# First two feed-forward layers: eight of 22 gate/up pairs as 2x2 blocks in seven products

## The reference

```
def swiglu(x, wi, wo):
    gate, up = jnp.split(x @ wi, 2, axis=-1)
    return (jax.nn.silu(gate) * up) @ wo
...
h = h + 0.5 * swiglu(rms_norm(h, ffn1_norm[li]), ffn1_wi[li], ffn1_wo[li])
```

## Time and profile before

| | us |
|---|---|
| median of 3 runs | 2762.38 (2761.88 to 2763.02) |
| the profiled execution | 2763.58, its span 2761.8 |
| PE busy | 2717.8 (98%), 14176 matmuls |
| PEld busy | 2210.9 (80%) |
| DVE busy | 1572.0 (57%) |
| ACT busy | 1205.9 (44%) |
| POOL busy | 622.4 (23%) |
| all loads | 255 MB, 92 GB/s over the span |

### The profile page before, as it was taken

The page is one execution under the profiler, slowest core; times in us unless marked ns, Lnnn a source line. Parts: engine busy times, 40 slices in busy tenths (PEclk is TensorE's granted clock), DMA queues, the critical chain, the costliest instruction groups (busy, mean ns, idle before and its releaser), DMA issues.

```text
span 2761.8 us, 39016 instructions
## 1 busy us (share of the span) xinstructions
PE 2717.8 (98%) x14176; PEld 2210.9 (80%) x14176; DVE 1572.0 (57%) x2421; ACT 1205.9 (44%) x1814; POOL 622.4 (23%) x607
## 2 busy tenths in 40 slices
PE   8999999999999999999999999999999999899998
PEld 6888888788888888887778888877888888777777
DVE  5444336544443575435965764348777777676664
ACT  4333232543322333223553333246655555457775
POOL 3000013100001351002733520013322222123232
PEclk9999999999999999999999999999999999999999
DMA  5333332233333464333204653322222222122222
GB/s 151 92 99 93 99 83 77 80 96 92 98 98 93 143 189 133 93 99 90 77 26 120 188 154 95 97 70 76 70 70 70 70 71 67 43 77 62 68 61 69
DMA packets 484827, 255.24 MB, mean 92 GB/s; under 512 B 17843, under 2 KB 478422, under 8 KB 484710
## 3 DMA queue, kind: packets, MB, share of 16 engines
q1 hardware_dynamic: 484534, 253.40, 32.0%
q10 hardware_dynamic: 176, 0.27, 0.0%
HBM read 251.51 MB, written 2.13 MB: 92 GB/s over the span
## 4 chain that ended last, share of the span: by engine, by line
PE 91%; DVE 6%; ACT 1%; POOL 1%; issue 1%; DMA 0%; DVEq 0%; SPq 0%; ACTq 0%; POOLq 0%
PE bank L259 73%; PE bank L1906 2%; PE bank L1937 1%; PE bank L1939 1%; PE bank L1938 1%; DVE w_lo L245 1%; DVE dsa_work L1603 1%; PE bank L2013 1%; PE bank L2821 1%; DVE small L1597 1%; PE bank L2813 1%; PE bank L2050 1%; PE bank L2846 1%; DVE gdn_blocks L2410 1%; PE bank L981 1%
## 5 line engine op out<-in xcount | busy, mean ns | idle before, releaser
L259 PE MATMUL bank<-x_hi,w_hi 128*128 128x512 f32 x2320 | 936.6, 404 | 8.5 <-DVE w_lo L245 4.8
L259 PE MATMUL bank<-x_hi,w_lo 128*128 128x512 f32 x2320 | 907.7, 391 | 0.0
L259 PE MATMUL bank<-x_lo,w_hi 128*128 128x512 f32 x2320 | 906.7, 391 | 0.6 <-DVE x_lo L586 0.6
L245 DVE TENSOR_TENSOR w_lo<-w_raw,w_hi 128x1024 fp32r<-128x1024 f32 x429 | 529.9, 1237 | 551.4 <-ACT w_hi L239 550.8
L239 ACT ACTIVATE w_hi<-w_raw 128x1024 fp32r<-128x1024 f32 x429 | 450.6, 1055 | 615.9 <-PE bank L259 567.1
L259 PEld LDWEIGHTS bank<-x_hi,w_hi 128*128 128x128 f32 x2320 | 437.1, 188 | 106.4 <-issue 15.3
L259 PEld LDWEIGHTS bank<-x_hi,w_lo 128*128 128x128 f32 x2320 | 436.2, 188 | 93.2
L259 PEld LDWEIGHTS bank<-x_lo,w_hi 128*128 128x128 f32 x2320 | 437.6, 189 | 87.5 <-issue 3.6
L435 POOL TENSOR_TENSOR sumsq<-sumsq,sq 128x512 f32<-128x512 f32 x56 | 91.7, 1638 | 1290.6 <-ACT sq L421 1290.0
L259 PE MATMUL bank<-h_hi,w_hi 128*128 128x512 f32 x768 | 298.9, 389 | 0.0
L259 PE MATMUL bank<-h_hi,w_lo 128*128 128x512 f32 x768 | 298.8, 389 | 0.0
(11 more groups left out here) (485 smaller groups left out, 3471.8 us busy)
## 6 DMA issues: line engine op xcount, KB each, us to landing
w_raw<-in_ffn_wi_dram SPq DMA_DIRECT2D x176, 512.0 KB, 3.8
w_raw<-in_ffn_wo_dram SPq DMA_DIRECT2D x64, 512.0 KB, 3.7
w_raw<-in_ada_w_dram SPq DMA_DIRECT2D x48, 512.0 KB, 4.9
w_raw<-in_a_w_in_dram SPq DMA_DIRECT2D x48, 512.0 KB, 4.0
w_raw<-in_b_w_in_dram SPq DMA_DIRECT2D x32, 512.0 KB, 4.1
w_raw<-in_ffn_wo_dram SPq DMA_DIRECT2D x32, 384.0 KB, 3.2
w_raw<-in_even_w_in_dram SPq DMA_DIRECT2D x16, 512.0 KB, 4.0
w_raw<-in_a_w_out_dram SPq DMA_DIRECT2D x16, 512.0 KB, 3.5
```

Of the source, the lines that this page charges most:

```text
L245: dve.tensor_tensor(w_lo[s][:], w_raw[raw_of(b) % RAW][:], w_hi[s][:].bitcast(F32), ALU.subtract).then_inc(w_lo_done, 1)
L259: mm = pe.matmul(out, lhs[:, w], rhs(kt), start=first and kk == 0 and m == 0, stop=last and kk == len(kts) - 1 and m == 2)
```

## The change

In ffn0 and ffn1, pairs 6 to 13 of 22 (SEVEN_AT = 6, SEVEN_N = 8) are computed as a product of 2x2 blocks. The weight side is split into gate/up by lower/upper four k-tiles, the token side into lower/upper four k-tiles by the first and last 256 tokens (T1, T2). Instead of eight block products seven are run, each of 4 k-tiles x 3 matmuls of 128x128 by 256 tokens (`seven_group`), on sums and differences of blocks. PE's order in a steady turn n is: products 5 and 2 of pair n, product 3 of pair n-1 (`last_pe`), products 1 and 7 of pair n+1 (`first_pe`, `seventh_pe`), and products 4 and 6 of pair n.

The work round it: DVE makes x_part = hres x gain x rstd in eight operations in the first turn of the loop (`parts_dve`); POOL makes four sums of its quarters, ACT and DVE split them into t_hi and t_lo. x_hi and x_lo are themselves rewritten with the parts of x_part in four steps (`own_act`, `own_dve`), the first one from the middle of the last dense block on; rstd then becomes 1. For each pair POOL makes four sums of weight halves, 128x512 each: both, three (in place), low (in place), all. ACT and DVE split left, both and all (512 columns) and row and low (1024 columns). ACT copies products 1 and 7 out of the bank (256 columns each) and applies Silu in two halves; DVE joins partial sums in banks and in prod. The raw loads of pair n+2 wait for these (`seven_sp`). Six dense pairs stand in front and eight behind, the first of these split round the last product 3. In the seven stretch the loops are written out. Two pairs move in the order of h tiles (`seven_col`), which the down product reads by the same map. The core of the diff:

```diff
+SEVEN = (0, 1)
+SEVEN_AT, SEVEN_N = 6, 8
+HT = T // 2
...
+        x_part, x_sum = tile("x_part", 4, KT), tile("x_sum", FT + 4, KT)
+        t_hi = [tile(f"t_hi{c}", FT + 14 + 2 * c, 2, F32R) for c in range(4)]
+        t_lo = [tile(f"t_lo{c}", 14 + 2 * c, 2, F32R) for c in range(4)]
+        w_both, w_all = tile("w_both", 13), tile("w_all", FT + 13)
+        p7_copy = [sumsq[:, 0:HT], sumsq[:, HT:T]]
...
         def ffn_pe(pe, f, run, r, begun=0):
             b0, t0 = BASE[f"ffn{f}"]
-            if not ada_of(f):
+            if f in SEVEN:
...
+                project_pe(pe, run, b0, t0, 4, r, begun)
+                for u in range(4, 2 * SEVEN_AT - 1):
+                    one(u)
+                one(2 * SEVEN_AT - 1, part=0, half=upper_read)
+                one(2 * SEVEN_AT - 1, part=1)
+                seven_pe(pe, f, one)
+                o = 2 * (SEVEN_AT + SEVEN_N)
+                for u in range(1, 4):
+                    one(o + u)
+                with pe.Fori(1, (2 * FT - o) // 4) as i:
+                    for u in range(4):
+                        one(o + u, i, 4)
+            elif not ada_of(f):
...
                     dve.tensor_tensor(prod[s][:], prod[s][:], gate_s[s][:], ALU.mult).then_inc(prod_done, 1)
+                    if f in SEVEN and turn0 == 0:
+                        parts_dve(dve, f, gain, range(4 * s, 4 * s + 4))
...
+        def seven_sp(sp, f, n, src):
...
+                if n >= 2:
+                    if m == 0:
+                        sp.wait_ge(all_added, c + 1)
+                        sp.wait_ge(row_lo, c + 1)
+                    else:
+                        sp.wait_ge(low_lo, c + 1)
...
+        def parts_dve(dve, f, gain, ks):
+            for k in ks:
+                x = slice(k * T, k * T + T)
+                dve.scalar_tensor_tensor(x_part[:, x], hres[:, x], gain[:, k:k + 1], rstd[:], ALU.mult, ALU.mult).then_inc(part_made, 1)
...
+        def parts_pool(pool, f):
...
+            pool.tensor_tensor(s22, b22, b12, ALU.subtract).then_inc(part_added, 1)
+            pool.tensor_tensor(s12, b11, b12, ALU.subtract).then_inc(part_added, 1)
+            pool.wait_ge(part_added, c + 1)
+            pool.tensor_tensor(s11, s22, b11, ALU.add).then_inc(part_added, 1)
+            pool.wait_ge(part_added, c + 3)
+            pool.tensor_tensor(s21, s11, b21, ALU.subtract).then_inc(part_added, 1)
...
+        OWN = ((0, T1), (1, T1), (1, T2), (0, T2))
+        def own_act(act, f, m):
...
+            act.activation(quarter(x_hi, k, t), quarter(x_part, k, t), ACT.Copy).then_inc(own_hi, 1)
...
+        def seven_group(pe, slot, h, x, out, first=False):
+            hi, lo = w_hi[slot], w_lo[slot]
+            x_h, x_l = x
+            for k in range(4):
+                w = slice(h * T + k * P, h * T + k * P + P)
+                for m, (lhs, rhs) in enumerate(((hi, x_h), (hi, x_l), (lo, x_h))):
+                    mm = pe.matmul(out, lhs[:, w], rhs[:, k, :], start=first and k == 0 and m == 0, stop=k == 3 and m == 2, skip_group_check=True)
+            return mm
...
+        def seven_pe(pe, f, one):
+            seventh_pe(pe, f, 0)
+            first_pe(pe, f, 0)
+            seventh_pe(pe, f, 1)
+            for n in range(SEVEN_N):
...
+                seven_group(pe, slot_of(f, 0), 0, part_pair(2), B[:, T1])
...
+                seven_group(pe, slot_of(f, 0), 1, own_pair(1, T1), A[:, T1]).then_inc(p2_done, 1)
+                if n:
+                    last_pe(pe, f, n - 1)
+                if n + 1 < SEVEN_N:
+                    first_pe(pe, f, n + 1)
+                    if n:
+                        seventh_pe(pe, f, n + 1)
+                pe.wait_ge(low_lo, c + 1)
+                pe.wait_ge(p7_joined, c + 1)
...
+                seven_group(pe, slot_of(f, 3), 0, part_pair(1), B[:, T1])
+                seven_group(pe, slot_of(f, 3), 1, part_pair(3), B[:, T2]).then_inc(p4_done, 1)
...
+            own_pe(pe, f, 3)
+            one(o, part=0)
+            last_pe(pe, f, SEVEN_N - 1)
+            one(o, part=1)
...
+        def seven_act(act, f):
...
+            own_act(act, f, 0)
+            own_act(act, f, 1)
+            both_act(act, f, 1)
+            copy_act(act, f, 0)
+            left_act(act, f, 1)
+            low_act(act, f, 0)
+            own_act(act, f, 2)
+            for n in range(SEVEN_N):
+                if n + 1 < SEVEN_N:
+                    row_act(act, f, n + 1)
...
+                first_silu(act, f, n)
+                all_act(act, f, n)
+                if n == 0:
+                    own_act(act, f, 3)
+                if n:
+                    last_silu(act, f, n - 1)
+                if n + 2 < SEVEN_N:
+                    left_act(act, f, n + 2)
+                if n + 1 < SEVEN_N:
+                    copy_act(act, f, n + 1)
+                if n:
+                    seven_h_hi(act, f, n - 1)
+                if n + 1 < SEVEN_N:
+                    low_act(act, f, n + 1)
+                if n + 2 < SEVEN_N:
+                    both_act(act, f, n + 2)
+                if n == 0:
+                    high(1)
+            next_hi(act, f, 1)
+            last_silu(act, f, SEVEN_N - 1)
...
+        def last_dve(dve, f, n):
...
+            dve.wait_ge(p4_done, seven(f) + n + 1)
+            dve.tensor_tensor(prod[s][:, T2], B[:, T1], p7_copy[n % 2], ALU.add).then_inc(last_joined, 1)
...
+        def join_dve(dve, f, n):
...
+            dve.tensor_tensor(B[:, T2], B[:, T1], p7_copy[n % 2], ALU.add).then_inc(p7_joined, 1)
...
+        def seven_dve(dve, f):
...
+            both_dve(dve, f, 0)
+            own_dve(dve, f, 0)
+            up(1)
+            product(1)
+            both_dve(dve, f, 1)
+            own_dve(dve, f, 1)
+            left_dve(dve, f, 1)
+            for n in range(SEVEN_N):
+                if n:
+                    last_dve(dve, f, n - 1)
+                low_dve(dve, f, n)
+                if n and n + 1 < SEVEN_N:
+                    both_dve(dve, f, n + 1)
+                join_dve(dve, f, n)
+                if n + 1 < SEVEN_N:
+                    row_dve(dve, f, n + 1)
...
+                if n == 0:
+                    own_dve(dve, f, 2)
+                all_dve(dve, f, n)
+                if n:
+                    up_dve(dve, f, n - 1)
+                if n == 0:
+                    own_dve(dve, f, 3)
+                if n + 2 < SEVEN_N:
+                    left_dve(dve, f, n + 2)
+                if n == 0:
+                    low(1)
+                else:
+                    h_lo_dve(dve, f, n - 1)
...
+        def seven_pool(pool, f):
+            parts_pool(pool, f)
+            for n in range(2):
+                both_pool(pool, f, n)
+                three_pool(pool, f, n)
+                low_pool(pool, f, n)
+                if n == 0:
+                    all_pool(pool, f, 0)
+            for n in range(SEVEN_N - 1):
+                all_pool(pool, f, n + 1)
+                if n + 2 < SEVEN_N:
+                    both_pool(pool, f, n + 2)
+                    three_pool(pool, f, n + 2)
+                    low_pool(pool, f, n + 2)
```

More of the change, by code:

```diff
@@ L106, in col, with seven_col @@
     return bass.ds(i * step, n * step)
+def seven_col(n):
+    return {SEVEN_AT - 2: 12, **{SEVEN_AT - 1 + k: 4 + k for k in range(8)}}.get(n, n)
 def first_and_second_block(nc, a, out):
@@ L198, in first_and_second_block @@
         ada_made, ada_added, ada_summed = sem("ada_made"), sem("ada_added"), sem("ada_summed")
+        part_made, part_added, part_hi, part_lo = sem("part_made"), sem("part_added"), sem("part_hi"), sem("part_lo")
+        left_hi, both_hi, row_hi, low_hi, all_hi = (sem(f"{n}_hi") for n in ("left", "both", "row", "low", "all"))
+        left_lo, both_lo, row_lo, low_lo, all_lo = (sem(f"{n}_lo") for n in ("left", "both", "row", "low", "all"))
+        both_added, three_added, low_added, all_added = (sem(f"{n}_added") for n in ("both", "three", "low", "all"))
+        p1_done, p7_done, p2_done, p3_done, p4_done = (sem(f"p{n}_done") for n in (1, 7, 2, 3, 4))
+        p1_copied, p7_copied, p7_joined, last_joined = (
+            sem(n) for n in ("p1_copied", "p7_copied", "p7_joined", "last_joined"))
+        own_hi, own_lo, rstd_ones, upper_read = sem("own_hi"), sem("own_lo"), sem("rstd_ones"), sem("upper_read")
         normed = sem("normed")
@@ L245, in split_lo, with products @@
             dve.tensor_tensor(w_lo[s][:], w_raw[raw_of(b) % RAW][:], w_hi[s][:].bitcast(F32), ALU.subtract).then_inc(w_lo_done, 1)
-        def products(pe, b, out, rhs_hi, rhs_lo, kts, first, last, i=0, n=0, part=None, parts=2, raws=None, low=None):
+        def products(pe, b, out, rhs_hi, rhs_lo, kts, first, last, i=0, n=0, part=None, parts=2, raws=None, low=None, half=None):
             if not part:
@@ L686, in ffn_pe, with one @@
             b0, t0 = BASE[f"ffn{f}"]
-            if not ada_of(f):
+            if f in SEVEN:
+                def one(u, i=0, n=0, part=None, half=None):
+                    if not part:
```

(27 more changed lines are left out.)

310 lines of the change are left out of this document (303 added, 7 removed).

## The result

The changed kernel takes 2769.33 us (median of 8 runs, 2768.09 to 2771.49), the kernel before on the same chip 2762.68 (8 runs, 2761.7 to 2763.12): ratio 1.0024, 95% interval 1.0016 to 1.0033. It is 6.65 us slower where 6.8 faster was forecast. The profiled execution took 2769.37, with a span of 2767.6 against 2761.8.

What follows compares the result with a forecast made beforehand. PE's issue pace was taken as the bound. Per layer 9.8 saved minus 4.5 entry, 1.7 clock and 0.2 exit gives 3.4 us, 6.8 for two: median 2755.6 us, likeliest 2750 to 2760, range 2743 to 2769.

Steps and rivals of the forecast that it cites:

- Columns: PE in the seven products: 0.115 us per 256-column matmul, 9.66 us a pair, saving 9.8 us a layer (6.4 to 10.9).
- Rival 3: Seven products: weight loads set PE's pace at 0.12 us, 10.08 a pair, no change at 2762 us; chance 0.14.
- The dense front: Dense pairs before the seven products: added x_part operations, sums and splits stay hidden; cost 0, bounds 0 and +1 (ffn0).
- The helpers in the steady middle: Steady turns: ACT 6.3, DVE 6.9, POOL 5.2 us a pair fit 9.66, arriving 1 to 4 us early; PE sets the pace.
- Rival 2: Steady turn: DVE and POOL become the bound through their shared port, up to 10.8 us a pair, 2774 us; chance 0.15.
- The entry: First seven-product pairs: queued steps idle PE, mainly 4.0 us before pair 0's last product; 4.5 a layer, bounds 0 and 7.
- The 0.5 forecast for the start: Start of each layer's seven products: PE waits 0.5 us for both_dve(1), before product 7 of pair 1.
- The clock: After the entry gap: 3.4 us at half clock, costing 1.7 us a layer, bounds 0 and 3.4.
- The exit: Return to dense blocks around the last product 3: 0.2 us a layer, bounds 0 and 1.

Runs made afterwards that it cites:

- e6: Changed kernel with the seven products run over 192 of their 256 tokens, same loads and instructions; 2762.46 us (one execution).
- e12: Changed kernel with POOL's four sums over half their columns, the rest set to zero; 2762.08 us (one execution).
- e4: Changed kernel with seven products in ffn1 only, ffn0 left dense; 2763.41 us, ratio 1.0002 to the kernel before.
- e5: Changed kernel with the seven products run over 240 of their 256 tokens, same loads and instructions; 2759.05 us (one execution).
- e1: Changed kernel with DVE's low(1) moved behind last_dve(0), the join PE waits for; 2765.37 us, ratio 1.0008.
- e7: Changed kernel with 15 unused matmuls on PE before its wait ahead of product 3 of pair 0, in each layer; 2764.82 us, ratio 1.0007.
- e10: e8 with part_dve(1) and part_dve(3) behind left_dve(1), parts in order 0, 2, 1, 3, and own_act(0) ahead of silu(1); 2761.27 us, ratio 0.9996.
- e13: e10 with part_dve(3) moved behind join(0) and awaited by product 6 only; 2759.69 us, ratio 0.9989.
- e11: e10 with own_dve(3) behind join(1), high(1) and low(1) moved into turn 1, left_dve(3) behind last_dve(1); 2763.29 us, ratio 1.0003.
- e2: Changed kernel with left_act(0) ahead of silu(0) and left_dve(0) ahead of gate(0); 2767.75 us, ratio 1.0021.
- e3: Changed kernel with the moves of e1 and e2 together; 2764.07 us, ratio 1.0008.
- e8: e3 with last_dve(0) ahead of left_dve(2), and low(1) behind both_dve(2) and join(1); 2762.17 us, ratio 0.9997.

## Why the prediction was wrong

Forecast -6.8 us, measured +6.65. By its own steps:

- **Columns, the first step that failed.** "Half of a dense one is 0.1133", and with pairs of single steps 0.11 and 0.12 the mean of 0.115 was taken. Measured 0.120, every one. The term of 9.8 a layer is 6.4, so 6.8 us of the 13.5 between forecast and measurement. The earlier trace rows already held the price: 0.2267 us for 512 columns is 512 columns at 2.4 GHz, 0.2133, and 0.0133 that don't scale. 256 columns are 0.1067 + 0.0133 = 0.1200. Halving the whole also halved the fixed part, which a pair of 84 matmuls pays 84 times and not 42.
- The Trainium skill, page "TensorE: Matmul & The Clock Gate", section "Back-to-back issue gap", gives the gap of an isolated matmul of N columns at the full clock as N / 2.4 plus 2.5 ns, and about 131 ns for 512 columns in a stream with a weight load each. The trace agrees with the form, not with the constant: 226.7 and 120.0 ns measured, 215.8 and 109.2 by the formula, 13.3 instead of 2.5. It doesn't agree with the 131 ns at all.
- **Rival 3 had the number and not the cause.** It priced 0.120 as the loads'. e6 shows the loads' floor at 0.1117; at 256 columns it is the columns. Its sum of no change, 6.4 - 6.4 a layer, was the nearest, and the two steps below put the loss on top.
- **The dense front, the second.** "Cost 0, bounds 0 and +1 (ffn0)". It was 3.5 us. The forecast counted the sums' own time (about 2.5 each; they took 2.4 to 3.9) and not what they do to DVE: 3.46 for 1.22 and 2.10 for 0.69, twice, is 5 us of lag. In the kernel before, these pairs are where a late DVE catches up, for a pair takes it 7.6 us there against PE's 10.88: its lag in ffn0 is 5.3 us at the fourth block's bank, 2.0 at the sixth and 0.2 at the eighth. In the changed kernel the x_part operations make it 9.3 us for a pair of the first turn and the held ones 12.5 for the next, so the lag is 6.9, 7.6 and 6.9, and the splits of the sums keep it at 7.0 till the eleventh bank. In ffn1 the same lags are 2.9, 3.5, 2.8 and 3.0: it starts 4 us less late, and has that slack at the entry. e12 shows the cause, e4 that the loss is ffn0's alone. The rule that the forecast set against the steady turn (the Trainium skill, "SBUF — State Buffer", "SBUF: two separate sides": the shared port pair is held for a whole instruction) is borne out here: the DVE operation of 3.46 us and the two of 2.1 end 1.1 and 0.55 us after the POOL sum that they met. It had to be applied at the front, where single instructions are longest.
- **The helpers in the steady middle**: right. No gap in any turn from the third on. DVE is busy 79%, not the 9 of 10 forecast, with 7.9 us a pair for the 6.9 counted. Rival 2 is refuted at this pace, and e5 shows that DVE would have followed the forecast 9.66 too: at 9.4 us a pair it has no idle time left, but PE doesn't wait. The price set on rival 2 was off by its own terms: where a pair saves 0.8 us the 6.4 of entry and exit is just paid, so it decides from 10.08, not "from about 10.4".
- **The entry**: mechanism and size right. 4.0 us before product 3 of pair 0, at both layers, released by DVE's join, behind low(1), behind ACT, behind POOL (3.5 to 4.6 forecast); e1 confirms it by taking it away. The 0.5 forecast for the start was 1.1 in ffn1; in ffn0 it merged with the first gap. That the size came out as the 4.0 taken is partly luck, since both ends moved. The forecast's list up to this gap leaves out product 6 of pair 0; with it, its own steps give 14.3 for its 14.7. In ffn1 PE gets there at 15.7 and goes on at 19.6, not 18.2.
- **The clock**: mechanism right (e7), size too small in ffn0: 2.7 and 2.4 against 1.7 for one, 1.3 in ffn1. Two gaps, two spells, and these last 6.8 us, not 3.4. The forecast took its 3.4 from gaps after 1300 us; the same trace has a spell of 6.8 us at 14.2.
- **The exit**: 0.2 forecast, 0.1 found (PE's starts around the last product 3).

The sum: pace 6.8, first gap 3.0 beyond the 0.5 of the forecast, clock in ffn0 3.4 (5.1 for 1.7), ffn1's start 0.6, minus 0.4 for its clock and 0.2 for the exits, is 13.2 of the 13.5 us between forecast and measurement.

Open: why ffn1's dense front absorbs the same stretches is read from the lags in the traces and was not tried by itself, by giving ffn0 an earlier start of DVE. Moving POOL's sums to another engine or splitting them finely was not tried either.

## What to carry to other kernels

Take the pace of a narrower instruction from two measured sizes, slope and constant, never by halving one. When an idle engine that shares a port is given long instructions, charge its neighbour for each of them where they run, and follow that lag to the next seam, even 20 us on. A deferred instruction is not gone: where the helpers were in debt here, a move brought a fifth to two fifths of the wait that it removed (e1, e10 in ffn0, e13) or nothing (e11), and the rest turned up at the next due time.

## What the runs showed of the hardware that was not expected

- Matmul step by columns at full clock, each with its own 128x128 load: 0.2267 us at 512 (one load per matmul there too), 0.1200 at 256, 0.1120 at 240, 0.1117 at 192. Slope and constant from 512 and 256 would give 0.1133 at 240, 0.0013 too much. At the lower clock 256 columns step 0.2133 (2.56 us for twelve), 256 columns at 1.2 GHz, with nothing left over.
- A DVE instruction of 1.22 us took 3.46 beside a POOL sum of 1024 columns; POOL's own took up to 3.85.
- Each PE idle time of 3.35 to 3.80 us in these layers was followed by 3.4 or 6.8 us at half clock, those of 2.7 (e2, e3) too, that of 2.55 (e8) not. Of four alike of 2.0 (e1, e3) one was and three weren't; of two alike of 1.9 in ffn1 one was (e11) and one wasn't (e10). Its length alone doesn't decide. Filling the second gap of both layers with matmuls that nobody reads (e7) gave 4.5 us back.
